# Loading an expert pair's table entries inside the pair, three in place of four, on TensorE and ScalarE

## The reference, cut to what matters

```python
y = jnp.zeros_like(t)
for e in range(N_EXPERTS):
    he = jax.nn.silu(t @ w_gate[e]) * (t @ w_up[e])
    y = y + combine[:, e:e + 1] * (he @ w_down[e])
```

## Time and profile before

| | |
|---|---|
| time, median of 3 runs | 1477.58 us (1471.93 to 1480.18) |
| the profiled execution's own time | 1476.57 us |
| its span, first to last instruction | 1474.7 us |
| TensorE busy | 1320.9 us, 90% of the span |
| VectorE, ScalarE, GpSimd busy | 571.8, 432.6, 407.8 us |
| moved by DMA | 448.05 MB, mean 304 GB/s |
| mean granted clock of TensorE | 0.963 |

### The profile page before, as it was taken

The page is one execution under the profiler, slowest core; times in us unless marked ns, Lnnn a source line. Parts: engine busy times, 40 slices in busy tenths (PEclk is TensorE's granted clock), DMA queues, the critical chain, the costliest instruction groups (busy, mean ns, idle before and its releaser), DMA issues.

```text
span 1474.7 us, 20943 instructions
## 1 busy us (share of the span) xinstructions
PE 1320.9 (90%) x7694; PEld 816.0 (55%) x7695; DVE 571.8 (39%) x1234; ACT 432.6 (29%) x693; POOL 407.8 (28%) x190
## 2 busy tenths in 40 slices
PE   7999998888999899998899898699997979889975
PEld 6886786433433398775233343289886853333422
DVE  5598655412121243545223222367007062322224
ACT  4554433311111146442111111145445331111110
POOL 5893652000000077050000000169964710000000
PEclk9999999999999999999899899999999999999998
DMA  9564569989999984439389999796635479999961
GB/s 356 202 202 174 187 229 342 373 369 409 426 430 427 402 291 156 172 121 427 129 352 417 403 430 427 301 342 234 216 126 214 170 310 408 379 409 423 428 263 78
DMA packets 89629, 448.05 MB, mean 304 GB/s; under 512 B 7804, under 2 KB 9768, under 8 KB 70952
## 3 DMA queue, kind: packets, MB, share of 16 engines
q1 hardware_dynamic: 85856, 445.87, 75.9%
q10 hardware_dynamic: 3656, 0.57, 0.3%
HBM read 445.38 MB, written 1.05 MB: 303 GB/s over the span
## 4 chain that ended last, share of the span: by engine, by line
PE 69%; DMA 12%; DVE 10%; issue 4%; ACT 3%; POOL 2%; ACTq 0%; SPq 0%; DVEq 0%; POOLq 0%
PE ps L430 67%; DMA ring_hi<-in_moe_w_up 7%; DMA ring_lo<-in_w_up 3%; POOL WLO L2564 1%; DMA ring_lo<-in_ada_w 1%; PE ps L895 1%; DVE Z L1980 1%; DVE Z L1968 1%; DVE Z L1981 1%; DVE Z L1979 1%; DMA ring_lo<-in_w_ckv 1%; PE ps L452 1%; POOL RS L2533 1%; ACT WHI L1362 0%; DVE ST L1809 0%
## 5 line engine op out<-in xcount | busy, mean ns | idle before, releaser
L2564 POOL TENSOR_TENSOR WLO<-ring_lo,WHI 128x1024 fp32r<-128x1024 f32 (+1 forms) x154 | 376.9, 2465 | 697.2 <-ACT WHI L1362 695.4
L430 PE MATMUL ps<-ring_lo,Z 128*64 128x512 f32 x1328 | 450.5, 622 | 30.9 <-issue 15.0
L430 PE MATMUL ps<-ring_hi,Z 128*64 128x512 f32 x1072 | 387.4, 613 | 22.8 <-issue 9.5
L430 PEld LDWEIGHTS ps<-ring_lo,Z 128*64 128x64 f32 x1328 | 141.2, 143 | 231.2 <-issue 213.5
L1362 ACT ACTIVATE WHI<-ring_lo 128x1024 fp32r<-128x1024 f32 (+1 forms) x160 | 166.3, 1049 | 208.6 <-PE ps L430 191.3
L430 PEld LDWEIGHTS ps<-ring_hi,Z 128*64 128x64 f32 x1072 | 117.8, 141 | 167.0 <-issue 161.4
L2231 DVE TENSOR_TENSOR Z<-ps,Z 64x512 f32<-64x512 f32 x48 | 33.1, 689 | 352.3 <-ACT Z L1569 349.1
L1569 ACT ACTIVATE Z<-ps 64x512 f32<-64x512 f32 x48 | 28.4, 591 | 365.1 <-PE ps L430 352.3
L430 PE MATMUL ps<-WHI,HTH 128*128 128x512 f32 x320 | 126.4, 395 | 5.0 <-DVE HTL L2433 1.6
L430 PE MATMUL ps<-WHI,HTL 128*128 128x512 f32 x320 | 125.1, 391 | 0.0
L430 PE MATMUL ps<-WLO,HTH 128*128 128x512 f32 x320 | 125.1, 391 | 0.0
(11 more groups left out here) (297 smaller groups left out, 1705.1 us busy)
## 6 DMA issues: line engine op xcount, KB each, us to landing
ring_lo<-in_moe_w_gate SPq DMA_DIRECT2D x25, 2048.0 KB, 15.5
ring_lo<-in_ada_w SPq DMA_DIRECT2D x24, 2048.0 KB, 9.2
ring_hi<-in_moe_w_up SPq DMA_DIRECT2D x23, 2048.0 KB, 16.7
ring_lo<-in_moe_w_down SPq DMA_DIRECT2D x17, 2048.0 KB, 15.9
ring_lo<-in_w_up SPq DMA_DIRECT2D x16, 2048.0 KB, 17.0
ring_hi<-in_moe_w_down SPq DMA_DIRECT2D x15, 2048.0 KB, 13.7
ring_lo<-in_ret_w_in SPq DMA_DIRECT2D x12, 2048.0 KB, 8.9
ring_hi<-in_w_gate SPq DMA_DIRECT2D x10, 2048.0 KB, 15.1
```

Source lines behind the costliest of these rows:

```text
L430: return nc.tensor.matmul(o, l, r, start=start, stop=stop, skip_group_check=True)
L2564: nc.gpsimd.tensor_tensor(WLO[:, q, 0:size], slot(r)[:, q * size:(q + 1) * size], WHI[:, q, 0:size].bitcast(F32), ALU.subtract).then_inc(S ...
```

## The change

TensorE and ScalarE no longer load two entries at the head of each `more`. They load three entries once in a pair: the numbers of extra blocks of both experts, and `b1` of the first. `b1` of the second is `b1` of the first plus the first's number of blocks, a register addition. TensorE does its three loads behind the gate and up products of both experts, ScalarE at the very start of the pair. The wait of TensorE for the table moves with them, from ahead of the first pair to ahead of the first loads.

```diff
@@ TensorE, pair(), behind the two gate_up
+                if first:
+                    pe.wait_ge(S("table"), L + 1)
+                blocks = [pe.value_load(TBL[0:1, L, 0, bass.ds(2 * p + a, 1)], min_val=0, max_val=3) for a in range(2)]
+                before = pe.value_load(TBL[0:1, L, 1, bass.ds(2 * p, 1)], min_val=1, max_val=48)
@@ TensorE, end of pair() and head of more()
                 down_half(banks[0], 1, wd)
                 for a in range(2):
-                    more(p, k, a, wg[a], wu[a], wd[a], final)
-
-            def more(p, k, a, wg, wu, wd, final):
-
-                e = 2 * p + a
-                nb = pe.value_load(TBL[0:1, L, 0, bass.ds(e, 1)], min_val=0, max_val=3)
-                b1 = pe.value_load(TBL[0:1, L, 1, bass.ds(e, 1)], min_val=1, max_val=48)
+                    more(p, k, a, blocks[a], before if a == 0 else before + blocks[0], wg[a], wu[a], wd[a], final)
+
+            def more(p, k, a, nb, b1, wg, wu, wd, final):
+
                 with pe.If(nb > 0):
@@ TensorE, ahead of the first pair
             gather_first()
-            pe.wait_ge(S("table"), L + 1)
             pair(0, 0, first=True)
@@ ScalarE, pair()
                 p = 2 * q + k
+                blocks = [act.value_load(TBL[0:1, L, 0, bass.ds(2 * p + a, 1)], min_val=0, max_val=3) for a in range(2)]
+                before = act.value_load(TBL[0:1, L, 1, bass.ds(2 * p, 1)], min_val=1, max_val=48)
                 silu(p, k, 0)
@@ ScalarE, end of pair() and head of more()
                 for a in range(2):
-                    more(p, a)
-
-            def more(p, a):
-
-                e = 2 * p + a
-                nb = act.value_load(TBL[0:1, L, 0, bass.ds(e, 1)], min_val=0, max_val=3)
-                b1 = act.value_load(TBL[0:1, L, 1, bass.ds(e, 1)], min_val=1, max_val=48)
+                    more(blocks[a], before if a == 0 else before + blocks[0])
+
+            def more(nb, b1):
+
                 with act.If(nb > 0):
```

## The result

| | before | after |
|---|---|---|
| median, first comparison | 1474.65 us (6 runs) | 1457.21 us (6 runs) |
| ratio, 95% interval | | 0.9879 [0.9858, 0.9901] |
| second comparison, on another chip | 1477.84 us (10 runs) | 1453.80 us (5 runs), 0.9838 [0.9815, 0.9861] |

The change makes the kernel faster by 1.2 to 1.6%, 17 to 24 us. The prediction was 1469.9 us, with 1463.5 as its lower end: a gain of 7.7 us was forecast, 17 to 24 came. The kernel before is not at one level in all comparisons (medians of 1473.31 to 1477.84 us), so kernels are best read by their ratios, each to the kernel before in its own comparison. Ratios and means leave out two executions of kernels further down that were in a slow state, 4643.37 us (changed kernel with a few filled waits) and 2676.37 us (twice as many loads).

A forecast was written before the change was run, and what follows sets the result against it. TensorE's late issue at long pair-end branches was taken to bound the kernel only where weight transfers don't; terms 2.0 + 0.8 + 3.1 + 1.8 = 7.7 us off 1477.58 gave 1469.9 us, range 1463.5 to 1478.5.

The forecast's parts named there:

- The block count: Pair-end branches: second skips crossing 256-instruction borders stay long at layer 0 pair 0, layer 1 pair 3, layer 2 pair 2.
- The stretch from the first branch to the end of the second: At long branches: stays about 6 us, since the instruction fetch hangs on the first branch, which comes 1.6 us earlier.
- rival B: Pair ends: long branches go altogether, by fetch beginning with the second branch or by new places; 1463.9 us, chance 0.12.
- TensorE's terms: Expert layers: 2.0 us in layer 0, 0.8 in layer 1, 3.1 in layer 2, 1.8 at layer 0's end; 7.7 us.
- The end of layer 0: Behind the last transfer: long branch 1.3 us sooner and half the scatter ahead of the last result; 1.8 us gain.
- Layer 1's pause of 0.8 us: Transfer pause at 843 to 846 us in layer 1, expected to go altogether; 0.8 us gain.
- the small one at 336 us: Small transfer pause in layer 0, expected to go; 0.5 us of layer 0's 2.0 us gain.
- Layer 2's term: Transfer pause at 1272 to 1277 us goes with the stall that made it, plus a smaller one; 3.1 us gain.
- Its loads lie in that hole, three instead of four ...: nothing: ScalarE between two pairs: its loads fall within an 11.86 us wait for TensorE, so moving them gains nothing.
- I count no clock gain where a gap of over 2 us remains: TensorE's clock behind long pair-end gaps: no gain counted there; layer 2's 2.3 us goes to a transfer-bound queue.
- Loads in the middle cost nothing: Behind the gate products: three loads take 2.4 us, hidden by the sequencer's 3.5 us lead; cost nothing.
- the wait for the table costs nothing: TensorE's table wait moves behind 14 us of products and was over before them; cost nothing.

The follow-up runs named there:

- changed kernel with a few filled waits: Changed kernel plus 2, 1 and 3 products without effect in TensorE's waits in the two executed extra blocks; 1454.09 us, ratio 0.9856.
- twice as many loads: Changed kernel with six TensorE loads in place of three behind each pair's gate and up products; 1459.24 us, ratio 0.9889.
- TensorE's part: Kernel before with only TensorE's loads changed, ScalarE's as before; 1465.07 us, ratio 0.9943.
- the kernel before with its code moved: Kernel before with 99 instructions of fulfilled waits at the head of TensorE's program; 1467.10 us, ratio 0.9952.
- the changed one with its loads at the end: Changed kernel with TensorE's three loads at the pair's end, ahead of both branches; 1459.30 us, ratio 0.9903.
- the old layout: Changed kernel with fulfilled waits added so that branches lie in the same blocks of 256 as in the kernel before; 1460.27 us, ratio 0.9899.

## Why the prediction was wrong

*The block count was right for the branches that it named.* The three stayed long, the others went, and moving the code by 99, 140 and 144 instructions moved them nearly as counted. (The count itself, 20,263 instructions in blocks of 256, stands in no trace; these runs are what bears it out.) It did not foresee the five of 2.8 to 3.7 us: for pair 1 of layer 1 it had up to 1 us, measured were 3.7. They cost little, as TensorE idles 0.98 us behind that one. At pairs 2 and 7 of layer 0 it had expected little change, and the branches are short there (0.21 us).

*The stretch from the first branch to the end of the second keeps its length: right.* So rival B falls in its first form. The packet with the instructions says the same: in these three it starts 3.5 to 4.3 us behind the first branch before and 4.0 to 4.5 after the change, but 1.5 to 2.5 us behind the second branch before and 3.5 to 4.1 after. The Trainium skill ("Runtime: NRT & Kernel Launch", section on instruction fetch mechanics) has the fetch begin with the branch whose target isn't there. The trace differs: the second branch of pair 0 in layer 0 was started 2.1 us earlier, 1.3 us of it relative to the first, and became 1.0 us longer.

*TensorE's terms.* Forecast 7.7 us, measured for TensorE's part 9.0, of which 7.0 at equal clock. In the changed kernel layer 0's last wait for a transfer ends 3.2 us earlier (489.71 to 486.56) against 2.0, but the 32 product records behind it take 8.77 us in place of 7.09, so 1.5 us are left at 498.21. The end of layer 0 gives 3.3 - 0.45 = 2.85 us of shorter idle time, of which 2.3 and 2.5 us pass on in the changed kernel's two profiles (0.9 with TensorE's part alone), against 1.8. Layer 1's pause of 0.8 us went, the small one at 336 us did not. Layer 2's term was mis-sized: up to pair 6 it gained 5.4 us (second branch of pair 0 to first of pair 6: 171.8 us before, 166.4 with TensorE's part) against 3.1. There the half-clock stretches behind the gaps at pairs 1 and 2 went too (0.61 and 0.55 in six us before; 1.00 in 1277 to 1392 us after). That milestone also parts layout and position: 166.9 us for the kernel before with its code moved, 167.5 for the changed one with its loads at the end, 169.3 with the old layout. So in layer 2 it was mostly the layout. Right in mechanism, a little small.

*"Its loads lie in that hole, three instead of four ...: nothing": the first step that failed.* It was read from the 11.86 us before ScalarE's first work of the next pair, an ordinary pair's end. In the two pairs with an extra block the next thing that ScalarE does is the copy inside that block, 1.6 us behind TensorE, and TensorE waits for it. The trace of before had the row (719.17, 1.60 <-ACT XROWS) and it was not read. Two blocks give 3.2 us of waiting, and 4.7 +- 3 were measured at equal clock; early loads in these two pairs alone give the whole. The sum also left out the pause of the transfers behind layer 1's extra block (share 0.36 in 747 to 756 us), which lost more than any that it counted and shrank by half.

*"I count no clock gain where a gap of over 2 us remains": the second.* It looked only behind the long gaps at pair ends. It held behind the gap of 2.18 us (0.72 in 305 to 311 us, as behind that of 4.02), but not at pair 2 of layer 2, where 2.95 us are left and the clock is 1.00 behind them (0.55 before). The clock is also low in the extra blocks, where waits of 1.4 to 3.1 us follow each other, and 1.6 us less there, or another set of holes elsewhere, changed the mean clock by 0.0095: some 9.5 us by the estimate above, half of the gain. In layer 1 the shorter wait went with the higher clock, in layer 2 only with TensorE's code as before, so the runs show a lower clock with the longer wait in those cases, and no rule. How many half-clock stretches a run has differs from one execution to the next (0.967 to 0.979 for the changed kernel in its first comparison, 1462.05 to 1451.69 us), so their part can't be read from one profile.

*Loads in the middle cost nothing, the wait for the table costs nothing: right,* up to six loads.

What stays open: how much of TensorE's 9 us is position and how much is layout, beyond 2 to 9 us each by the ratios and nothing clear of noise at equal clock; why the changed kernel's clock is low in layer 2's extra block; why a few microseconds of idle time in one place cost more clock than in another.

## What to carry to other kernels

When work of a helper engine is moved, look at every place where that engine is next waited for, rare paths (here an extra block that runs twice) first; an idle time of 12 us at the common place says nothing about them. A short wait in a chain of short waits can cost more than its length if TensorE's clock falls there (6.0 us for 1.6 in layer 1 here): compare busy time for the same number of products, and the mean clock over several runs, before counting a wait at its face value. Where branches skip long bodies, count where the borders of the instruction blocks fall, as any edit ahead of them moves them; adding waits at the program's head moved them too and held the first product up by 4 to 9 us. And take more than one profile: code that was not touched differed by up to 2.7 us between two.

## What the runs showed of the hardware

- Mean clock and time: 0.99 +- 0.11 us for 0.001. 0.001 of the clock is 2 x 0.001 x 1470 = 2.9 us at 1.2 in place of 2.4 GHz, so a microsecond at half clock cost 0.34 us here. The Trainium skill ("TensorE: Matmul & The Clock Gate", section on terms) puts the penalty at the throttled time times one minus the clock's share, that is half of it here; by the runs it is less. That part of such time is idle or hidden behind transfers would account for it, but was not measured.
- A product of 128x64 by 128x512 in float32 makes two records of 0.44 us where it stands alone; two that write different halves of the output's rows run side by side (a gate and an up product start 0.01 us apart at 504.02 us, a pair every 0.43 us).
- 99 instructions of two fulfilled waits each at the program's head held the first product up by 4.3 us (11.49 to 7.18), 140 by 8.7; 144 spread over the projections by none that shows (7.24).
- A branch that is not taken is 70 ns and most taken ones are 0.2 to 0.4 us. Where the first of two skips enters a new block of 256 instructions and the second leaves it again, the second takes up to 6.8 us, and over these kernels the longest end 5.9 to 7.2 us behind the start of the first.
- Where the 32 records of down products behind a wait for a transfer take 7.09 us at one time they take 8.77 at another: the granted clock is 1.00 over the first and 0.81 over the second (layer 0's last ones, kernel before and changed kernel).
